# Row spreads and the memory decay as one rounded product over high and low parts, gate copies ahead of the maxima

## The chip, the cores and the metric

One core of one Trainium2 chip runs the whole program. The time is the device time of one execution in microseconds (us). Engines: PE (TensorE, matrix products), DVE (VectorE), ACT (ScalarE), POOL (GpSimd), SP (SyncE, which only issues the loads of weights here). Products accumulate in PSUM; all other tiles lie in SBUF.

## The reference, cut to what matters

256 tokens and 256 context tokens, width 1024, float32. A first block: modulated norm, one wide projection, windowed attention beside an mLSTM memory, a gated merge, a convolved FFN. A second block: a "fox" (forgetting) attention and a stick-breaking attention, FFN, a convolutional mixer, FFN. What the change touches:

```
q = rope(rms_norm(aq, q_norm_w));  k = rope(rms_norm(ak, k_norm_w))      # first attention: 1/rms per head and token
dmat = b[t] - b[s] + i[s];  m_t = max(b + m, dmat.max());  s = (q k^T) * exp(dmat - m_t)    # mLSTM
q, k = rms_norm per head (second attention, fox and stick-breaking)
y = sigmoid(ga) * (att @ wa) + sigmoid(gm) * (ml @ wm)
```

An rms factor exists once per head and token, as a row of 256 (token) values on the partition of its head; it is needed on all 64 partitions of the head. The "memory decay" is, per head, direction and token, minus the running maximum of `i[s] - b[s]`, needed on all 128 partitions. Both spreads are made by a matrix product with a selecting 0/1 operand.

## The kernel before, in words

Every weight block (128x1024) is loaded by SP into a ring `raw`, split into a rounded high part `whi` by ACT (L1145) and a rounded low part `wlo` by POOL (L313, one tensor_tensor of 128x1024 that reads SBUF and writes SBUF). PE multiplies with three rounded (fp32r) matmuls in place of one exact product (L482 to L484). In the FFNs some of the low parts are made by DVE.

Each engine has one stream of instructions, written out by hand and ordered by semaphores.

The projection blocks are called q = 0 to 59 (`W_IN_JOBS`); blocks 20 to 27 are the attention's queries, 28 to 35 the output gates ("mo"), 36 to 43 "ga", 44 to 51 "gm". On PE, `gp_job(q)` makes a block's product in a PSUM bank; on ACT, `evac(q)` copies it away and then makes the next high part. All "mo" and all "gm" products use bank 0, so `gp_job` of one waits for `evac` of the one before it. On DVE, `evac(q)` of a query block is followed by `rotated`.

Stage "memory" (h = 0 to 4, about 190 to 252 us). PE: `decay_rows(h)` (L673, two exact f32 products of 256 columns), `ml_scores(h)` (L683), `gp_job(28+2h)`, `ml_values(h-1)` (L703), `gp_job(29+2h)`. DVE: exponents from the decay (L1796, L1799), products with the scores (L1806, L1810), then in h = 0 the rms rows (L1763 to L1765) and `make_spread` (L1743), in h = 3 a second `make_spread`, then `combine(h-1)` (L1773 to L1785). ACT: exponentials (L1283), `evac(28+2h)`, an exponential (L1286); from h = 1 on it waits for the end of `combine(h-1)`, squares its result twice (L1292) and only then does `evac(29+2h)`. `ml_scores(h)` waits for DVE's products of h-1.

Stage "first spreads" (252 to 290 us). PE for i = 0 to 9: `spread_first(i)` (L744, an exact f32 product, 512 columns for i < 2, else 256), from i = 2 on `gp_job(36+i-2)`, from i = 4 on two transposes (L727). DVE multiplies by the result (L1855).

Stage "attention" (16 steps st, 290 to 373 us). PE: scores (L770, L774), the "gm" product in the steps of `GM_AT` (1, 3, 5, 7, 9, 11, 15, 16), transposes of the step before (L785), in odd steps values (L796) and reciprocals (L807). DVE: maxima (L1870), copies (L1879), and in even steps the output (L1893), which waits for ACT's L1333. ACT in step st: two exponentials (L1322, L1324), `evac` of the "gm" block of step st-1 with its split, then in even steps L1333.

Stage "second heads" (660 to 820 us). DVE, after the norm: `make_spread(spread2)` and seven more small preparing operations (L2054 to L2060), each followed by a wait for its own end (`link`); then it copies the values out of PSUM (L2139) once PE has made them. PE for j = 0 to 15: `project(j)`, at j = 1 the forget gates, from j = 6 on `spread_rstd(j-6)` (L924, exact, 256 columns), from j = 1 on `head_sums(j-1)` (L914), from j = 8 on stick-breaking scores (L959, L960), from j = 9 on `sb_later` (L968 to L971). `head_sums(0)` waits for the four copies L2139; `project(2)` for DVE's copy of `project(0)` (L2160). `row_rstd(g)` on DVE (L1576 to L1580, with ACT's L1431 and L1434) makes the rms rows of four blocks at j = 5, 9, 13 and after the loop; `forget_sums` comes at j = 6. Afterwards come the fox heads (L1010 to L1016, maxima L2118, L2127, transposes L1028), with spreads 10 and 11 ahead of them and 12 to 15 among heads 2 and 3.

Of the kernel before, what the change touches and what calls it, by code (L numbers as in the profile page):

```python
# [12 lines left out]
P = 128  # L13
# [112 lines left out]
def build(nc, xc_d, ccol_d, params_d, const_d, const1_d, const2_d, wgate_d, wf_d, stream_d, out_d):  # L126
# [3 lines left out]
    with ctx:  # L130
# [25 lines left out]
        spr = NG[:, :, :].rearrange("p a t -> p (a t)")  # L156
# [75 lines left out]
        def wait_rest(eng, s):  # L232
# [13 lines left out]
            "spread_ready", "v_chain", "v_ones", "rot_fin", "rows_read", "c_across", "modb_done",  # L246
# [173 lines left out]
        turned_cos = [work[:, 1024 + 256 * i:1280 + 256 * i] for i in range(4)]  # L420
        def spread_of(rows, b):
            return KX[0:rows, C1_COS + P * b:C1_COS + P * b + P] if b < 5 else spr[0:rows, P * (b - 5):P * (b - 4)]
# [34 lines left out]
        spread2 = KX[:, C2_N:2 * C2_N]  # L457

        def fin_out(i):

            return PS[:, 4 + i % 2, T:2 * T] if i < 8 else PS[:, 0 if i < 12 else i % 2, 0:T]
# [18 lines left out]
        def _(pe):  # L480
# [183 lines left out]
            def decay_rows(h):  # L664

                if h >= 1:
                    pe.wait_ge(S["ctx_exp"], 4 * h)
                    pe.wait_ge(S["arg_done"], 4 * h)
                else:
                    pe.wait_ge(S["em_done"], 1)  # L670
                for d in range(2):
                    r = 32 * d + h
                    mm = pe.matmul(PS[:, 1, T * d:T * d + T], ident[0:36, r:r + 1].broadcast_to((36, P)),  # L673
                                   NG[0:36, 0, :], start=True, stop=True)
                mm.then_inc(S["bc_done"], 1)
# [56 lines left out]
            def spread_first(i):  # L732

                if i >= 2:
                    pe.wait_ge(S["qk_fin"], i - 1)
                else:
                    pe.wait_ge(S["spread_ready"], 2)
                    pe.wait_ge(S["rq_done"], 2)
                if i < 2:
                    rows, sel, n = ROWS[0:4, 256:768], spread_of(4, i), 2 * T  # L740
                else:
                    b = i - 2
                    rows, sel, n = ROWS[0:16, 0:256], spread_of(16, b), T
                pe.matmul(PS[:, 2 + i % 2, 0:n], sel, rows,  # L744
                          start=True, stop=True).then_inc(S["rstd_bc"], 1)
# [171 lines left out]
            def spread_rstd(i):  # L917

                g, b = i // 4, i % 4
                pe.wait_ge(S["rq_done"], 3 + g)  # L920
                pe.wait_ge(S["spread_ready"], 3)
                if i > 8:
                    pe.wait_ge(S["qk_fin"], 10 + fin_before(i) + 1)
                pe.matmul(fin_out(i), spread2[0:8, P * b:P * b + P], rr2[2 + g][0:8, :],  # L924
# [207 lines left out]
        def _(act):  # L1132
# [182 lines left out]
            for st in range(STEPS + 3):  # L1315
                if st < STEPS:
# [9 lines left out]
                if st - 1 in GM_AT:  # L1326
                    evac(GM0 + GM_AT[st - 1])
# [212 lines left out]
        def _(dve):  # L1540
# [7 lines left out]

            cos, sin = KX[:, C1_COS:C1_COS + T], KX[:, C1_SIN:C1_SIN + T]
# [174 lines left out]
            for q in range(MO):  # L1724
# [10 lines left out]
                if q > AQ:  # L1735
                    rotated(q - AQ + 1)
            rotated(9)
# [3 lines left out]
            def make_spread(to, first, blocks, n=16):  # L1741

                dve.tensor_copy(to[0:n, 0:P * blocks].rearrange("r (h d) -> r h d", d=HD),  # L1743
                                ident[0:n, 2 * first:2 * first + 2 * blocks].unsqueeze(2)
                                .broadcast_to((n, 2 * blocks, HD))).then_inc(S["spread_ready"], 1)
# [43 lines left out]
            for h in range(5):  # L1789
# [23 lines left out]
                if h == 0:  # L1813
                    row_norms()
                    make_spread(KX[:, C1_COS:C1_N], 0, 5)
                if h == 3:
                    make_spread(spr, 5, 3)
# [222 lines left out]
            def row_rstd(g):  # L2040
# [3 lines left out]
                dve.wait_ge(S["rq_done"], 3 + g)  # L2044

            make_spread(spread2, 0, 4, 8)
# [341 lines left out]
```

## Time and profile before

| | us |
|---|---|
| median of 3 runs (1326.45 to 1329.6) | 1327.8 |
| profiled execution | 1325.02 |
| its span, first to last instruction | 1323.2 |
| busy in the span: PE | 1266.8 |
| PE weight loads | 1155.2 |
| DVE | 785.6 |
| POOL | 701.9 |
| ACT | 629.3 |
| mean granted TensorE clock | 0.977 of full |

Busy times are sums over the span; times inside it are counted from its start. Granted clock 1.0 is 2.4 GHz, 0.5 is 1.2 GHz. An exact f32 matmul stands in the rows as two instructions (x2), a rounded one as one.

### The profile page before, as it was taken

The numbers are of one execution on the slowest core, as the hardware profiler recorded it, in microseconds if no ns is written. First come the engines' busy times: TensorE is split into PE (matmuls) and PEld (weight loads), VectorE is DVE, ScalarE is ACT, GpSimd is POOL, SyncE is SP. The second block draws the span as 40 slices with busy tenths as digits, with TensorE's granted clock in tenths as the row PEclk, the third lists the DMA queues.
The fourth block names the chain that finished last, engine by engine and source line by source line (L and its number), as shares of the span: only waits on it lengthen the run. The fifth ranks groups of instructions, "written<-read, shape, count | busy, mean of one in ns | idle before, by whom it ended". The sixth has DMA issues, their size and how long they took to land.

```text
span 1323.2 us, 24847 instructions
## 1 busy us (share of the span) xinstructions
PE 1266.8 (96%) x9248; PEld 1155.2 (87%) x9248; DVE 785.6 (59%) x1432; ACT 629.3 (48%) x1081; POOL 701.9 (53%) x299
## 2 busy tenths in 40 slices
PE   5789999999999899999898999999999999999999
PEld 1578888876699799999887857999999999999998
DVE  3688567535631467776546652577776424677775
ACT  3523343454543655555634522655555644654553
POOL 1536663252248555557585301655558787655564
PEclk9899999999999899999999977999999999999999
DMA  9568662141135444556463300455546456355552
GB/s 373 199 229 272 242 195 80 49 128 49 49 93 164 127 161 176 187 190 217 127 191 112 93 20 5 140 190 190 180 176 218 148 187 190 129 189 190 189 179 78
DMA packets 57739, 208.45 MB, mean 158 GB/s; under 512 B 6576, under 2 KB 7600, under 8 KB 57408
## 3 DMA queue, kind: packets, MB, share of 16 engines
q1 hardware_dynamic: 57168, 205.55, 46.2%
q0 software_dynamic: 496, 1.87, 0.4%
q8 instruction: 50, 0.82, 0.2%
q14 instruction: 25, 0.20, 0.1%
HBM read 206.35 MB, written 1.05 MB: 157 GB/s over the span
## 4 chain that ended last, share of the span: by engine, by line
PE 88%; DVE 6%; DMA 3%; issue 2%; ACT 2%; SPq 0%; DVEq 0%; ACTq 0%
PE ps L482 24%; PE ps L483 23%; PE ps L484 23%; DMA raw<-in_stream 3%; PE ps L703 2%; PE ps L517 2%; PE ps L519 2%; PE ps L520 2%; PE ps L547 1%; PE ps L796 1%; PE ps L1016 1%; PE ps L770 1%; DVE raw L1645 1%; PE ps L924 1%; PE ps L785 1%
## 5 line engine op out<-in xcount | busy, mean ns | idle before, releaser
L313 POOL TENSOR_TENSOR wlo<-raw,whi 128x1024 fp32r<-128x1024 f32 x286 | 696.1, 2451 | 583.1 <-ACT whi L1145 557.1
L482 PE MATMUL ps<-Hh,whi 128*128 128x256 f32 (+2 forms) x1976 | 577.6, 292 | 20.2 <-DVE Hl L1611 4.7
L483 PE MATMUL ps<-Hl,whi 128*128 128x256 f32 (+2 forms) x1976 | 568.7, 288 | 0.0
L484 PE MATMUL ps<-Hh,wlo 128*128 128x256 f32 (+2 forms) x1976 | 568.5, 288 | 0.0
L482 PEld LDWEIGHTS ps<-Hh,whi 128*128 128x128 f32 (+1 forms) x1976 | 382.0, 193 | 34.1 <-issue 14.9
L1145 ACT ACTIVATE whi<-raw 128x1024 fp32r<-128x1024 f32 x338 | 353.3, 1052 | 114.4 <-DMA raw<-in_stream 57.2
L483 PEld LDWEIGHTS ps<-Hl,whi 128*128 128x128 f32 (+1 forms) x1976 | 382.3, 193 | 3.1
L484 PEld LDWEIGHTS ps<-Hh,wlo 128*128 128x128 f32 (+1 forms) x1976 | 382.0, 193 | 2.7
L2000 DVE SCALAR_TENSOR_TENSOR arena<-ps,sm,arena 128x255 f32<-128x255 f32 (+1 forms) x264 | 127.4, 483 | 103.8 <-ACT arena L1395 95.9
L482 PE MATMUL ps<-dh,whi 128*128 128x256 f32 x592 | 167.6, 283 | 1.1 <-DVE dl L1912 1.1
L483 PE MATMUL ps<-dl,whi 128*128 128x256 f32 x592 | 167.5, 283 | 0.0
L484 PE MATMUL ps<-dh,wlo 128*128 128x256 f32 x592 | 167.5, 283 | 0.0
L1395 ACT ACTIVATE arena<-ps,sm 128x256 f32<-128x256 f32 x132 | 66.7, 505 | 134.5 <-DVE ps L1990 104.1
L482 PEld LDWEIGHTS ps<-dh,whi 128*128 128x128 f32 x592 | 113.7, 192 | 1.3 <-issue 1.3
L483 PEld LDWEIGHTS ps<-dl,whi 128*128 128x128 f32 x592 | 113.7, 192 | 0.0
L484 PEld LDWEIGHTS ps<-dh,wlo 128*128 128x128 f32 x592 | 113.7, 192 | 0.0
L1962 DVE COPY sm<-params 128x8 f32 (+1 forms) x66 | 89.1, 1355 | 7.9 <-DVE arena L2000 7.6
L1973 DVE TENSOR_TENSOR wlo<-raw,whi 128x1024 fp32r<-128x1024 f32 x52 | 81.0, 1557 | 1.5
L1406 ACT ACTIVATE dh<-ps 128x256 fp32r<-128x256 f32 x60 | 23.1, 385 | 100.7 <-DVE ps L2009 100.7
L1645 DVE SCALAR_TENSOR_TENSOR raw<-raw,arena 128x1024 f32<-128x1024 f32 x32 | 57.7, 1830 | 3.9 <-DMA raw<-in_stream 3.6
L517 PE MATMUL ps<-whi,Hh 128*128 128x512 f32 (+1 forms) x128 | 47.4, 370 | 4.0 <-DVE Hl L1632 4.0
L519 PE MATMUL ps<-whi,Hl 128*128 128x512 f32 (+1 forms) x128 | 47.2, 368 | 0.0
(298 smaller groups left out, 1249.0 us busy)
## 6 DMA issues: line engine op xcount, KB each, us to landing
raw<-in_stream SPq DMA_DIRECT2D x386, 512.0 KB, 4.1
X<-in_xc SPq DMA_DIRECT2D x2, 1024.0 KB, 10.4
out_y<-X SPq DMA_DIRECT2D x8, 128.0 KB, 2.0
kx<-in_const POOLq DMA_DIRECT2D x1, 512.0 KB, 7.0
arena<-in_wgate POOLq DMA_DIRECT2D x1, 400.0 KB, 8.9
params<-in_params POOLq DMA_DIRECT2D x1, 372.0 KB, 6.9
k<-in_const POOLq DMA_DIRECT2D x1, 256.0 KB, 4.9
kx<-in_const POOLq DMA_DIRECT2D x1, 256.0 KB, 4.6
```

The costliest lines, as they stand in the source:

```text
L313: pool.tensor_tensor(wlo[:, slot, :], raw[:, rslot, :], whi[:, slot, :].bitcast(f32), ALU.subtract).then_inc(rest_done[0], 1)
L482: pe.matmul(out, lh, rh, start=start, stop=False, skip_group_check=True)
L483: pe.matmul(out, lh, rl, start=False, stop=False, skip_group_check=True)
L484: return pe.matmul(out, ll, rh, start=False, stop=stop, skip_group_check=True)
L517: pe.matmul(out, Hh[:, k, tok], wh_, start=k == 0 and first, stop=False, skip_group_check=True)
L519: pe.matmul(out, Hl[:, k, tok], wh_, start=False, stop=False, skip_group_check=True)
L1145: act.activation(whi[:, s % RING, :], raw[:, r % RING, :], ACT.Copy).then_inc(hi_done, 1)
L1395: act.activation(tc, PS[:, 4 + 2 * slot + j, 0:T], ACT.Identity, bias=bias, scale=cwb[:, slot, 3 * j:3 * j + 1]).then_inc(S["centre"], 1)
L1645: dve.scalar_tensor_tensor(raw[:, r % RING, :], raw[:, r % RING, :], 1.0, c_across, ALU.mult, ALU.mult, accum_out=MODB[:, at:at + 1]).then ...
L1962: dve.tensor_copy(cwb[:, i % 2, :], src).then_inc(S["cw_copy"], 1)
L1973: dve.tensor_tensor(wlo[:, s % RING, :], raw[:, RAW_OF_W[s] % RING, :], whi[:, s % RING, :].bitcast(f32), ALU.subtract).then_inc(rest_done ...
L2000: dve.scalar_tensor_tensor(tc[:, lo:hi], u[:, src:src + hi - lo], cwb[:, slot, 3 * j + 1 + n:3 * j + 2 + n], tc[:, lo:hi], ALU.mult, ALU.a ...
```

## The change

Three things. (1) Row operands of the three kinds of spreads are split by DVE into a rounded high part and the rounded rest, stacked on two groups of partitions of a cleared fp32r tile, and the selecting operand is doubled likewise, so that each spread is one rounded product. (2) For this, DVE clears and fills tiles: two clears, three copies and a subtract in query block 21; three clears, two copies and two subtracts in h = 0; in h = 1 and h = 2 two clears, four copies and a small memset each, ahead of `combine`; ahead of the second heads six clears and four copies in place of one copy; a copy and a subtract behind each `row_rstd`. `cleared`, and all copies except those of `spread_rows`, wait for their own end. (3) ACT's `evac` of a "gm" block stands ahead of the two exponentials of its step.

```diff
+        decay, decay_of = Hl[0:100, 4, T:2 * T], Hh[0:100, 3, T:T + 36]
+        k_rows, q_rows = Hl[0:36, 5:7, T:2 * T], Hl[0:48, 7, T:2 * T]
         def spread_of(rows, b):
-            return KX[0:rows, C1_COS + P * b:C1_COS + P * b + P] if b < 5 else spr[0:rows, P * (b - 5):P * (b - 4)]
+            return Hh[0:rows, 4 + b // 2, T + P * (b % 2):T + P * (b % 2) + P]
...
-        spread2 = KX[:, C2_N:2 * C2_N]
+        head_rows = [dh[0:40, 0, :], dh[0:40, 1, :], dl[0:40, 0, :], dl[0:40, 1, :]]
+        spread2 = [Hl[0:40, k, T:2 * T] for k in (0, 3)]
...
-                    pe.wait_ge(S["em_done"], 1)
+                    pe.wait_ge(S["decay_split"], 1)
...
-                    mm = pe.matmul(PS[:, 1, T * d:T * d + T], ident[0:36, r:r + 1].broadcast_to((36, P)),
-                                   NG[0:36, 0, :], start=True, stop=True)
+                    mm = pe.matmul(PS[:, 1, T * d:T * d + T], decay_of[:, r:r + 1].broadcast_to((100, P)),
+                                   decay, start=True, stop=True)
...
-                    pe.wait_ge(S["rq_done"], 2)
+                    pe.wait_ge(S["rows_split"], 2)
...
-                pe.wait_ge(S["rq_done"], 3 + g)
-                pe.wait_ge(S["spread_ready"], 3)
+                pe.wait_ge(S["heads_split"], 1 + g)
+                pe.wait_ge(S["spread_ready"], 6)
...
-                pe.matmul(fin_out(i), spread2[0:8, P * b:P * b + P], rr2[2 + g][0:8, :],
+                pe.matmul(fin_out(i), spread2[b // 2][:, P * (b % 2):P * (b % 2) + P], head_rows[g],
...
             for st in range(STEPS + 3):
+                if st - 1 in GM_AT:
+                    evac(GM0 + GM_AT[st - 1])
                 if st < STEPS:
...
-                if st - 1 in GM_AT:
-                    evac(GM0 + GM_AT[st - 1])
...
+            def cleared(out, like):
+                link(dve.tensor_scalar(out, like, 0.0, None, ALU.mult))
+            def spread_rows(rows, out, heads):
+                n = heads.stop - heads.start
+                dve.tensor_copy(out.rearrange("r (h d) -> r h d", d=HD),
+                                ident[rows, heads].unsqueeze(2).broadcast_to((rows.stop - rows.start, n, HD)))\
+                   .then_inc(S["spread_ready"], 1)
+            def split_rows(hi, lo, rows, done):
+                link(dve.tensor_copy(hi, rows))
+                dve.tensor_tensor(lo, rows, hi.bitcast(f32), ALU.subtract).then_inc(done, 1)
...
+                if q == AQ + 1:
+                    cleared(decay, K0[0:100, 0:T])
+                    cleared(decay_of, K0[0:100, 0:36])
+                    for rows in (slice(0, 36), slice(64, 100)):
+                        link(dve.tensor_copy(decay_of[rows, :], ident[rows, rows]))
+                    split_rows(decay[0:36, :], decay[64:100, :], NG[0:36, 0, :], S["decay_split"])
...
                 if h == 0:
                     row_norms()
-                    make_spread(KX[:, C1_COS:C1_N], 0, 5)
-                if h == 3:
-                    make_spread(spr, 5, 3)
+                    for k in (5, 6, 7):
+                        cleared(Hl[0:48, k, T:2 * T], K0[0:48, 0:T])
+                    for to, src in (((Hl[r, 5:7, T:2 * T] for r in (slice(0, 4), slice(32, 36))),
+                                     ROWS[0:4, 256:768].rearrange("r (b t) -> r b t", b=2)),
+                                    ((Hl[r, 7, T:2 * T] for r in (slice(0, 16), slice(32, 48))), ROWS[0:16, 0:256])):
+                        split_rows(*to, src, S["rows_split"])
+                if 1 <= h <= 2:
+                    for k in (2 * h + 2, 2 * h + 3):
+                        cleared(Hh[0:48, k, T:2 * T], K0[0:48, 0:T])
+                        for rows in (slice(0, 16), slice(32, 48)):
+                            at = rows.start + 4 * (k - 4)
+                            link(dve.tensor_copy(Hh[rows, k, T:2 * T].rearrange("r (h d) -> r h d", d=HD),
+                                                 ident[rows, at:at + 4].unsqueeze(2).broadcast_to((16, 4, HD))))
+                    dve.memset(rows_read, 0.0).then_inc(S["spread_ready"], 1)
                 if h >= 1:
                     combine(h - 1)
...
                 dve.wait_ge(S["rq_done"], 3 + g)
-
-            make_spread(spread2, 0, 4, 8)
+                split_rows(head_rows[g][0:8, :], head_rows[g][32:40, :], rr2[2 + g][0:8, :], S["heads_split"])
+
+            for out in (*head_rows, *spread2):
+                cleared(out, K0[0:40, 0:T])
+            for i in range(2):
+                for at in (0, 32):
+                    spread_rows(slice(at, at + 8), spread2[i][at:at + 8, :], slice(at + 4 * i, at + 4 * i + 4))
```

## Rows read from the trace of the kernel before

**Rows 1.** The page: the chain that ended last, by engine.
```profile
PE 88%; DVE 6%; DMA 3%; issue 2%; ACT 2%; SPq 0%; DVEq 0%; ACTq 0%
```

**Rows 2.** The chain in order of time: start us, us, what.
```profile
217.23 1.92 PE ps L683 x8
...
260.40 0.62 PE ps L744 x2
...
315.08 0.12 PE ps L484
```

**Rows 3.** Timeline of DVE, PE and POOL, 660 to 690 us: start, duration, instruction, [idle before].
```profile
660.63 2.36 DVE L2056 CAST Hh<-k 8x8 fp32r<-8x8 f32 x1
667.80 4.81 DVE L2060 TENSOR_SCALAR Hh<-k 128x256 fp32r<-128x256 f32 x2
678.95 2.48 DVE L2139 COPY arena<-ps 128x512 f32<-128x512 f32 x4 [6.34 <-PE ps L520]
...
687.25 0.60 PE L914 MATMUL ps<-arena,k 128*8 128x256 f32 x2
...
660.57 28.45 POOL L313 TENSOR_TENSOR wlo<-raw,whi 128x1024 fp32r<-128x1024 f32 x12 [14.22 <-ACT whi L1145]
```

**Rows 4.** Timeline of DVE, all operands in SBUF, POOL idle (708, 712, 200 us).
```profile
708.31 0.28 DVE L2071 TENSOR_SCALAR arena<-arena 8x256 f32<-8x256 f32 x1
711.79 0.41 DVE L2075 TENSOR_TENSOR Hh<-arena,Hh 8x256 fp32r<-8x256 f32 x1
...
200.83 0.68 DVE L1764 TENSOR_TENSOR arena<-arena 4x512 f32<-4x512 f32 x1
```

**Rows 5.** Timeline of the memory stage, 203 to 220 us.
```profile
204.09 0.39 PE L482 MATMUL ps<-Hh,whi 128*128 128x256 f32 x1 [1.10 <-ACT arena L1237]
...
203.60 0.48 DVE L1743 COPY kx<-k 16x640 f32<-16x640 f32 x1
...
215.09 0.87 DVE L1785 SCALAR_TENSOR_TENSOR X<-ps,sm,X 128x256 f32<-128x256 f32 x2
...
216.95 0.36 ACT L1237 ACTIVATE arena<-ps 128x256 f32<-128x256 f32 x1
```

**Rows 6.** Windows: busy us of PE, PEld, DVE, ACT, POOL, then granted clock.
```profile
651.30:655.10 3.80, 0.00 (x0) 0.00 (x0) 3.07 (x8) 1.63 (x4) 0.00 (x0) 1.00 0.00 0
656.40:659.60 3.20, 3.20 (x10) 2.48 (x8) 3.06 (x10) 1.95 (x6) 0.00 (x0) 0.53 0.00 0
775.00:790.00 15.00, 15.00 (x50) 10.28 (x50) 6.33 (x18) 2.32 (x11) 0.00 (x0) 0.52 0.01 2
```

**Rows 7.** Waits of PE, 290 to 372 us: who waited for whom, us, times, longest.
```profile
PE ps L482 <- ACT arena L1237: 2.7, 5, 0.5
PE ps L796 <- DVE arena L1893: 1.4, 1, 1.4
```

**Rows 8.** Timeline of ACT, attention, 320 to 325 us.
```profile
320.89 0.69 ACT L1322 ACTIVATE arena<-ps,sm 128x512 f32<-128x512 f32 x1 [4.26 <-DVE rows L1870]
...
322.87 1.06 ACT L1145 ACTIVATE whi<-raw 128x1024 fp32r<-128x1024 f32 x1
```

**Rows 9.** Timeline of PE, DVE and POOL, second heads, 706 to 728 us.
```profile
713.36 0.36 PE L482 MATMUL ps<-Hh,whi 128*128 128x256 f32 x1 [1.48 <-DVE arena L2160]
...
725.71 0.67 PE L968 MATMUL ps<-arena,kx 128*128 128x256 f32 x2 [0.70 <-DVE arena L2091]
...
725.01 0.55 DVE L2091 TENSOR_TENSOR arena<-arena,kx 128x384 f32<-128x384 f32 x1
...
725.13 2.68 POOL L313 TENSOR_TENSOR wlo<-raw,whi 128x1024 fp32r<-128x1024 f32 x1 [2.65 <-ACT whi L1145]
```

**Rows 10.** The chain: spreads 12 and 13 of the fox heads.
```profile
780.15 2.00 PE ps L924 x4
```

**Rows 11.** Timeline of PE, a later fox head.
```profile
799.20 0.90 PE L1028 MATMUL ps<-k,arena 128*128 128x128 f32 x3 [1.37 <-DVE arena L2127]
```

**Rows 12.** Timeline of DVE, query block 22.
```profile
168.54 0.48 DVE L1712 SCALAR_TENSOR_TENSOR arena<-ps,sm,kx 128x256 f32<-128x256 f32 x1 [1.21 <-ACT arena L1246]
```

More of the change, by code:

```diff
@@ L155, in build @@
         NG = sb("ng", [P, 2, T])
-        spr = NG[:, :, :].rearrange("p a t -> p (a t)")
         PS = ctx.enter_context(nc.psum_tensor("ps", [P, 8, 512], f32))
@@ L245, in build @@
             "sb_arg", "sb_wm", "fox_max", "fox_pt", "fox_even", "t2_lo", "mix_cu", "fin", "wg_lo",
-            "spread_ready", "v_chain", "v_ones", "rot_fin", "rows_read", "c_across", "modb_done",
+            "spread_ready", "decay_split", "rows_split", "heads_split", "v_chain", "v_ones", "rot_fin", "rows_read", "c_across", "modb_done",
             "c_bc", "mod_t", "mod_copy", "ss_ready", "gates_ps", "u_t", "st_done", "bc_done", "qk_done", "pv_done", "rot_done", "rstd_bc", "sc_done",
@@ L737, in spread_first @@
                     pe.wait_ge(S["spread_ready"], 2)
-                    pe.wait_ge(S["rq_done"], 2)
+                    pe.wait_ge(S["rows_split"], 2)
                 if i < 2:
-                    rows, sel, n = ROWS[0:4, 256:768], spread_of(4, i), 2 * T
+                    rows, sel, n = k_rows, spread_of(36, i), 2 * T
                 else:
                     b = i - 2
-                    rows, sel, n = ROWS[0:16, 0:256], spread_of(16, b), T
+                    rows, sel, n = q_rows, spread_of(48, b), T
                 pe.matmul(PS[:, 2 + i % 2, 0:n], sel, rows,
@@ L1739, in _ @@
             dve.tensor_tensor(MODB[:, :], MODB[:, :], pr("b_mod", 2 * KC, 6 * KC), ALU.add).then_inc(S["modb_done"], 1)
[L1741 to L1745, printed above, removed]
             ROW_SETS = ((4, 7, 2 * T, 256), (16, 6, T, 0))
```

## The prediction

> **What bounds the kernel now.** I read the chain that ended last by engine, then PE's waits, then the timelines around every edit. PE holds 88% of the chain [rows 1]; it is the bound nearly everywhere, and a product taken from it is worth its own length. The exceptions are a few places where PE waits for DVE, and every edit that adds to DVE must be read against those. Two things decide this case. First, DVE operations whose operands all lie in SBUF do not run while POOL makes a low part: an 8x8 copy took 2.36 us, and two clears of 128x256 took 4.81, all inside an unbroken run of 12 POOL operations (28.45 us, 2.37 each) [rows 3]; the same kinds take 0.28 to 0.68 us with POOL idle [rows 4]. Second, after PE stood idle for 3.8 us the granted clock fell to 0.53 in the stretch that followed, the 1.2 GHz level, against 1.0 [rows 6].
>
> **Part 1, what a spread saves.** An exact spread of 256 columns holds PE for 0.62 us on the chain, a rounded matmul of 256 columns for 0.12 [rows 2]. One change of operand type more or less goes with it, so between exact neighbours I take 0.41 saved. Where both neighbours are rounded (spreads 2 and 3 of the first attention) I take 0.69. Bounds for each: 0.31 (half of the exact product saved) and 0.69.
>
> **Part 2, query block 21.** DVE gets a clear, a small clear, two small copies, a copy and a subtract: about 1.3 us unblocked by rows 4. DVE has 1.21 us idle before the next block's first operation [rows 12]. At least one POOL operation (2.4 us) lies in the way. PE needs that block's copy some 3 us after it is normally made. I take +0.6; bounds 0 (one POOL operation) and +3.0 (two more).
>
> **Part 3, the memory stage.** The decay product of h = 0 saves nothing: the scores behind it wait for DVE's last rotation anyhow. That of h = 1 saves nothing either: PE waits 1.10 us at 204.09 for a copy of ACT that waits for the rms rows of DVE [rows 5]. Those of h = 2 and 3 save 0.8 each. Against this, DVE in h = 0 gets three clears at 0.31 (0.93), a copy of 512 (0.4), a subtract of 512 (0.7), a copy (0.3) and a subtract (0.4), less the removed copy (0.4 to the next operation): +2.4, with the links +2.7. The block by a POOL operation that the stage has anyway only changes its place. In h = 1 come two clears and four copies at 0.31: 1.9, and 0.6 for the rest of a POOL operation that is under way then. So `combine(0)`, whose last operations begin at 215.09, comes 2.7 + 2.5 = 5.2 us later. Behind it on ACT stand two squares and `evac(31)`, which comes at 216.95 [rows 5], and PE's block 32 waits for that. PE reached block 32 at 219.15 (217.23 + 1.92, [rows 2]), so the copy, done at 217.3, had 1.8 us to spare. Net +3.4 at block 32, and PE stands idle 3.7 us there. The same pattern in h = 2 has the lateness of DVE (again 1.9 more, less the 2 us it waited for PE) against a PE that is late itself: I keep +3.2 in all, the savings of h = 2 and 3 taken up by the waits. Bounds: -1.6 (all additions hidden, two decays saved) and +6 (a further POOL operation in the way twice, less half). For the idle 3.7 us I add 1.6 of low clock, the 3.2 us of rows 6 at half speed; bounds 0 and 3.2.
>
> **Part 4, first spreads.** Spreads 0 and 1 stand beside a chain of DVE (combine, multiply) and save nothing. Spreads 2 to 9 stand on the path: 6 x 0.41 + 2 x 0.69 = -3.8. Cover: DVE (0.4 to 1.3 us) and POOL (2.4) have under 3 us of work per block of 3.9. Bounds -2.5 and -5.0. The make_spread removed in h = 3 is off the path.
>
> **Part 5, gate copies.** PE waited five times, 2.7 us in all, for the copy out of bank 0, and once 1.4 us for L1893 [rows 7], which stood behind ACT's L1333, which stood behind the copy and its split. ACT is idle 4.26 us ahead of the exponentials of an even step; the copy and split take about 1.3 [rows 8], and the product they wait for is done by then. Both waits go, of the second 1.2, since DVE is ready for L1893 only 0.2 earlier than PE needs it: -2.7 - 1.2 = -3.9. Next to come late is nothing: with them gone PE is busy all through. Bounds -4.1 and, should a copy wait for its product and hold the exponentials back, +1.3 once.
>
> **Part 6, ahead of the second heads.** This is the largest term. DVE reaches the place at 659.91. Before, eight small operations followed, two of the seven linked ones ahead of POOL's run, five blocked; they ended at 672.6, and DVE then stood idle 6.34 us until the value products were ready at 678.95 [rows 3]. Now there are 17: three clears pass before POOL starts at 660.57; three clears, four copies and the old seven operations, 14 in all, meet a run of 12 POOL operations. One passes behind each POOL operation (five rows in a row show it): 12 x 2.39 = 28.7 us from 660.8, then two unblocked, so DVE is free at about 690.0. The four copies L2139 take 2.48 [rows 3], so `head_sums(0)` starts at 692.5 instead of 687.25: +5.2. If the four unlinked copies pass together, 11 are blocked, and it is +2.7 (no row shows unlinked ones under a run of POOL; one by one is the nearest, rows 3, and I take it). Bounds: 0 and +7. PE idle for 5.2 us brings the low clock again: +1.6, bounds 0 and +3.2.
>
> The Trainium skill, page "SBUF — State Buffer", section "Who interferes with whom", says that DVE and GpSimd share one pair of SBUF ports as an exclusive lock, taken for a whole instruction by whichever issues first, by DVE's copy, cast and tensor_scalar when everything is in SBUF and by a two-input operation against a GpSimd operation that reads. The trace agrees, down to the 8x8 copy of 2.36 us. A reader who took only the sizes of the added operations (some 3 us in all at this place) would find them hidden under the 6.34 us of idle time, and the sum below would be 6.8 lower.
>
> **Part 7, spreads of the second heads.** (a) j = 5, 6: DVE's chain from the first rms rows to L2160 sets PE's start at 713.36, a wait of 1.48 [rows 9]. A copy and a subtract, 0.3 + 0.41, lie on it: +0.8. The shift can put the last operations of `forget_sums` behind the next POOL operation: then +3.3. These are within 0.1 us of each other, so I take +2.1. (b) j = 9: PE waits 0.70 for L2091, which starts at 725.01, 0.12 ahead of a POOL operation; pushed 0.7 later, with POOL's start pulled ahead by the shorter spread, it falls behind it and ends 1.65 later [rows 9]: +1.65, bounds +0.3 and +2.4. (c) Spreads 4 to 9: 6 x -0.41 = -2.5, and +0.2 for j = 13, where DVE had 0.9 us to spare: -2.3, bounds -3.5 and -0.5. (d) Spreads 10 to 15: 10 saves 0.4; the fourth split adds 0.7 ahead of the first maxima; 12 and 13 hold PE 2.00 at 1.2 GHz [rows 10] and save 1.45; 14 and 15 covered a latency that elsewhere shows as a wait of 1.37 [rows 11], so they save 2.0 - 1.37 = 0.6. Sum -1.8, bounds -3.5 and 0.
>
> **Sum.** 0.6 + 3.2 + 1.6 - 3.8 - 3.9 + 5.2 + 1.6 + 2.1 + 1.65 - 2.3 - 1.8 = +4.15. The profiled execution took 1325.0 (span 1323.2 and 1.8 around it); it becomes 1329.2. It lay 2.8 below the median of 1327.8, so the median becomes 1332.0.
>
> **Rivals.**
> (A) DVE's additions are hidden: parts 3 and 6 cost nothing, because operations slip in between POOL's or their order in time turns out luckier. For it: DVE is busy only 59% of the span, and 6.34 us are idle in front of L2139. Against it: five operations in a row that did not slip in. It decides where DVE is free before 678.95, some 7 blocked operations after 660.57, instead of 14. Price: part 6 gone (-6.8), part 3 at -1.6 instead of +4.8 (-6.4): 1332.0 - 13.2 = 1318.8. This is the case on the faster side.
> (B) Half of it: the unlinked copies pass together (-2.5) and no low clock follows the stall in the memory stage (-1.6): 1327.9, no change.
> (C) The races with POOL go badly: part 7a at 3.3 (+1.2), part 2 at 3.0 (+2.4), low clock twice as long in both stalls (+3.2): 1338.8. For it: every DVE operation in SBUF is exposed to POOL's 2.4 us.
> (D) The gate copies do not help, since ACT waits in them for products or raw blocks: part 5 at 0 with the rest as forecast: 1335.9. Against it: 4.26 us idle at the place.
>
> **How the numbers follow.** Forecast 0.45, A 0.20, B 0.17, C 0.13, D 0.05. The likeliest is 1332.0, its own range 1328.5 to 1336. The range for 8 in 10 reaches down to A and up towards C: 1319 to 1338. A difference under 0.2%, 2.7 us, is what a measurement of this kernel can't tell from none. Slower: C, D and nearly nine tenths of the forecast, 0.57; same: B's most part and the rest of the forecast, 0.21; faster: A and a little of B, 0.22.
>
> **What would show it.** Right: L744, L673 and L924 as single instructions; no wait of L482 for L1237 among the attention's steps; a wait of PE of about 3.7 us for L1237 near 219 us; DVE operations of 2.4 us in unbroken order from 660 to 689 us, L2139 near 690 and a wait of `head_sums` of about 5 us; granted clock 0.5 behind both. Wrong: L2139 still at 679, `evac(31)` before PE reaches block 32, or added DVE operations of 0.3 us during POOL's. Parts 4 and 5 are wrong if the stretches 255 to 290 and 297 to 372 us do not shorten by 3.8 and 3.9.

## The result and the profile after

The changed kernel took 1332.24 us (median of 8 runs, 1330.07 to 1334.29); the kernel before, beside it, 1326.91 (8 runs, 1323.62 to 1329.60). The ratio is 1.0042, with a 95% interval of 1.0029 to 1.0055: slower by 0.4%. The forecast was 1332.0. It was a change of +4.15 put on a kernel of 1327.8, the median of three executions; measured side by side the change is +5.3. The profiled execution took 1330.07, with a span of 1327.8 against 1323.2. It is the fastest of the eight: its mean granted clock is 0.971, that of the others 0.964 to 0.969.

The chain of the page, by engine, now reads (to [rows 1]):

```profile
PE 84%; DVE 10%; DMA 3%; issue 2%; ACT 1%; SPq 0%; DVEq 0%; ACTq 0%
```

DVE's part of it grew from 6% to 10% and PE's fell from 88% to 84%: PE's products got shorter, and its waits for DVE longer. To place it, I took the start of the same PE instruction in both traces and noted how much later (+) the changed kernel is there:

| stretch (us of the span before) | later at its start | at its end | change | forecast |
|---|---|---|---|---|
| query block 21 (168 to 173) | -0.22 | +0.74 | +0.96 | +0.6 |
| memory stage (191 to 252) | +0.72 | +4.73 | +4.0 | +4.8 |
| first spreads (252 to 289) | +4.73 | +0.73 | -4.0 | -3.8 |
| attention (289 to 359) | +0.73 | -4.27 | -5.0 | -3.9 |
| ahead of the second heads (648 to 691) | -4.46 | +2.64 | +7.1 | +6.8 |
| second heads, j = 4 to 8 (7a) | +2.64 | +1.28 | -1.4 | +2.1 |
| j = 9 (7b) | +1.28 | +5.19 | +3.9 | +1.65 |
| j = 10 to 15 (7c) | +5.19 | +3.69 | -1.5 | -2.3 |
| the fox heads (7d) | +3.69 | +3.71 | 0.0 | -1.8 |

The last 0.9 us lie behind the last product, mostly in the output's transfers, which the change doesn't touch: from that product's start to the end of the span it is 4.4 us instead of 3.6.

**Ahead of the second heads.** The timelines of DVE, PE and POOL, changed kernel, 655 to 689 us (start, duration, instruction, idle before it; to [rows 3]):

```profile
655.46 0.60 DVE L1554 TENSOR_SCALAR dh<-k 40x256 fp32r<-40x256 f32 x2
656.09 2.70 DVE L1554 TENSOR_SCALAR dl<-k 40x256 fp32r<-40x256 f32 x2
658.83 4.78 DVE L1554 TENSOR_SCALAR Hl<-k 40x256 fp32r<-40x256 f32 x2
663.65 9.60 DVE L1559 CAST Hl<-k 8x256 fp32r<-8x256 f32 x4
...
685.67 2.48 DVE L2175 COPY arena<-ps 128x512 f32<-128x512 f32 x4
...
688.31 1.01 PE L917 MATMUL ps<-arena,k 128*8 128x256 f32 x2 [5.49 <-DVE arena L2175]
...
656.11 28.79 POOL L312 TENSOR_TENSOR wlo<-raw,whi 128x1024 fp32r<-128x1024 f32 x12 [14.23 <-ACT whi L1148]
```

Three clears pass at 0.3 us; from 656.4 on each clear, copy and rounding takes 2.3 to 2.4, the length of one POOL operation. The four copies, which don't wait for each other's end, do so too (9.60). Of the 14 operations that remained 12 were held, one per POOL operation, and the last two took 0.3 each. The copy out of the value banks starts at 685.67, not at 678.95 - 4.46 = 674.5, and PE stands 5.49 us. The windows behind it (busy time of PE, PEld, DVE, ACT and POOL, then the granted clock) show the 1.2 GHz level and the return to 2.4:

```profile
688.30:691.50 3.20, 3.19 (x12) 2.35 (x13) 0.52 (x2) 0.00 (x0) 0.00 (x0) 0.50 0.03 14
692.00:695.20 3.20, 3.20 (x25) 2.63 (x25) 0.42 (x1) 1.33 (x2) 0.20 (x1) 1.00 0.00 0
```

The head sums of j = 0 come 5.52 us later against before than the projections, those of j = 1 another 1.58.

**The memory stage.** The same timelines at 216 to 224 us (to [rows 5]):

```profile
216.91 0.80 DVE L1554 TENSOR_SCALAR Hh<-k 48x256 fp32r<-48x256 f32 x1
...
219.45 0.16 DVE L1793 SCALAR_TENSOR_TENSOR sm<-ps,emT 128x4 f32<-128x4 f32 x1
220.85 0.87 DVE L1805 SCALAR_TENSOR_TENSOR X<-ps,sm,X 128x256 f32<-128x256 f32 x2
...
222.70 0.36 ACT L1240 ACTIVATE arena<-ps 128x256 f32<-128x256 f32 x1
...
223.12 0.38 PE L485 MATMUL ps<-Hh,whi 128*128 128x256 f32 x1 [3.84 <-ACT arena L1240]
```

The clears and constant copies of h = 1 stand in front of `combine(0)`; its last operations begin at 220.85, not 215.09, and ACT's copy out of block 31's bank at 222.70, not 216.95: 5.8 later (forecast 5.2). PE's block 32 starts at 223.12 instead of 218.80, 4.3 later: it had 1.5 us to spare.

**First spreads.** The chain of the changed kernel has one such piece per spread of 256 columns (start, us, what):

```profile
263.32 0.31 PE ps L747
277.49 0.31 PE ps L747
```

A window between the third and the fourth spread, of the kernel before:

```profile
257.00:259.00 2.00, 2.00 (x11) 2.00 (x11) 2.00 (x4) 1.97 (x2) 0.00 (x0) 0.50 0.00 0
```

The same stretch of the changed kernel:

```profile
260.00:262.00 2.00, 2.00 (x16) 1.87 (x17) 1.83 (x7) 1.94 (x4) 0.00 (x0) 1.00 0.03 8
```

And of experiment 2, whose code up to this place is the changed kernel's:

```profile
261.00:264.00 3.00, 3.00 (x14) 2.87 (x15) 2.83 (x8) 2.94 (x4) 0.00 (x0) 0.56 0.00 0
```

A rounded spread holds PE 0.31 us where the exact one held it 0.62 [rows 2], so each saves 0.31: from the third spread to the tenth the distance to the kernel before changes by just that, eight times. Between the third and the fourth it changes by another 1.5: before, a stretch at 1.2 GHz lay there, and in the profiled execution of the changed kernel it doesn't. That is no effect of the change. Of the twelve kernels profiled for this document eleven have the stretch, among them experiments 2, 4 and 10, which up to there are the changed kernel, with the same wait of PE in front (2.7 us in all four).

**Attention.** PE's waits (290 to 372 us before, 290 to 368 us changed; to [rows 7]; who waited for whom, us, times, longest): the five waits for the copy out of bank 0 are gone, and so is the one for L1893. The first row is the kernel before, which had the wait for the first queries too; the second is the changed kernel's only row.

```profile
PE ps L770 <- DVE Hl L1843: 1.5, 1, 1.5
PE ps L773 <- DVE Hl L1874: 1.5, 1, 1.5
```

**The second heads.** Timelines of PE, DVE and POOL, changed kernel, 716 to 730 us (to [rows 9]):

```profile
716.76 0.35 PE L485 MATMUL ps<-Hh,whi 128*128 128x256 f32 x1 [2.10 <-DVE arena L2196]
...
729.33 1.04 PE L971 MATMUL ps<-arena,kx 128*128 128x256 f32 x2 [3.03 <-DVE arena L2127]
...
727.37 1.81 DVE L2127 TENSOR_TENSOR arena<-arena,kx 128x384 f32<-128x384 f32 x1
...
726.41 2.35 POOL L312 TENSOR_TENSOR wlo<-raw,whi 128x1024 fp32r<-128x1024 f32 x1 [2.34 <-ACT whi L1148]
```

Windows of the kernel before:

```profile
713.00:716.40 3.40, 3.04 (x17) 3.07 (x18) 0.98 (x3) 0.00 (x0) 2.23 (x1) 0.66 0.39 133
716.40:719.00 2.60, 2.60 (x13) 1.74 (x12) 0.00 (x0) 0.33 (x2) 0.00 (x0) 0.79 0.53 189
```

Windows of the changed kernel, the same place and behind the wait of j = 9:

```profile
713.00:716.40 3.40, 1.66 (x10) 0.90 (x9) 3.18 (x7) 1.33 (x2) 2.02 (x2) 1.00 0.28 88
...
729.00:732.60 3.60, 3.27 (x14) 3.13 (x15) 2.24 (x6) 0.52 (x1) 0.00 (x0) 0.57 0.45 146
```

DVE reaches its operation at j = 9 (L2127) 0.96 us behind POOL's start, where before it was 0.12 ahead; PE's wait grows from 0.70 to 3.03. The stretch of low clock that before lay at 713 to 719 is absent, and one follows the new wait at 729. The absence is again not the change's doing: experiments 2 and 3, which at this place have the changed kernel's code and its wait of 2.10, have the stretch. In experiment 1, which here is the kernel before, it comes some microseconds earlier (granted 0.52 from 704 to 706), ahead of the wait for DVE, and costs PE nothing. The stretch at 729 stands behind each of the seven waits of 3.0 us that were profiled at j = 9.

### The profile page after: what moved, and what is told of

The parts are those of the page before. It is cut to its first block, busy times and chain, and to the rows that moved or that the text cites. A ratio compares the mean times of both kernels' runs of the same rounds, so it can differ in the third digit from the quotient of the medians.

```text
span 1327.8 us, 24817 instructions
## 1 busy us (share of the span) xinstructions
PE 1253.7 (94%) x9214; PEld 1150.7 (87%) x9214; DVE 819.6 (62%) x1474; ACT 629.0 (47%) x1081; POOL 700.4 (53%) x299
## 3 DMA queue, kind: packets, MB, share of 16 engines
q0 software_dynamic: 496, 1.87, 0.3%
## 4 chain that ended last, share of the span: by engine, by line
PE 84%; DVE 10%; DMA 3%; issue 2%; ACT 1%; SPq 0%; DVEq 0%; ACTq 0%
PE ps L485 23%; PE ps L486 23%; PE ps L487 22%; DMA raw<-in_stream 3%; PE ps L706 1%; PE ps L550 1%; PE ps L773 1%; PE ps L799 1%; PE ps L520 1%; PE ps L523 1%; PE ps L522 1%; PE ps L788 1%; PE ps L1019 1%; DVE raw L1664 1%; DVE Hl L1559 1%
```

## The experiments

My theory: two costs, each a wait for DVE's added work, ahead of the second heads (5.5 us and 1.6 of low clock) and in the memory stage (3.8 and 1.6), and a third at j = 9; the gate copies gain 5 us, the spreads 0.31 each. The rivals: the waits have another releaser, or the added work is hidden as its size suggests. Ratios are against the kernel before, timed beside each.

**1. The gate copies alone, in the kernel before.**
```
 step(st) of ACT:
+    if st - 1 in GM_AT: evac(GM0 + GM_AT[st - 1])
     ... (the maxima's part)
-    if st - 1 in GM_AT: evac(GM0 + GM_AT[st - 1])
```


> The kernel before with the gate copies ahead of the exponentials and nothing else. Theory: PE's five waits for the copy out of bank 0 (0.5 us each, and 0.2 us for the first product after each) and the 1.4 us wait for the output both go, as between the traces of before and after, where this stretch became 5.0 us shorter: 1321.9 us, 5.0 below the kernel before; the trace of 290 to 372 us has no wait of PE for ACT's copy. The forecast's own term was 3.9 us. Rival: the stretch gained only because the spreads ahead of it had changed its start against the loads and low parts; then alone it gives under 2 us.

Measured 1321.65, ratio 0.9965 (0.9951 to 0.9978). In the attention the place against before moves from +0.31 to -4.66: -5.0, all of what the changed kernel gains there. PE's waits, 290 to 368 us:

```profile
PE ps L770 <- DVE Hl L1843: 1.5, 1, 1.5
```

So this edit alone makes the kernel faster, and the rest of the change costs some 10 us. Of the 5.0 the profiled span keeps 3.6: at j = 9 this kernel loses 1.5 us to a stretch of low clock (-5.18 to -3.65), in code that its edit doesn't touch.

**2. The second heads' preparation spread over j = 1 to 4** (in the changed kernel).
```
-            for out in (*head_rows, *spread2): cleared(out, ...)
-            for i in range(2): for at in (0, 32): spread_rows(...)
+            def prepare_heads(j):      # called behind the copy of q2 in step j
+                if j in (1, 2): three of the six clears
+                if j in (3, 4): two of the four spread_rows
```


> The changed kernel with the preparation of the second heads (six clears, four copies) moved from ahead of the seven old operations to behind the copies of projections 1 to 4. Theory: the seven linked operations then end near 670 us as before, the copies L2139 start when the value products are ready (about 674 us in this kernel's time), the 5.5 us wait of head_sums and 1.6 us of low clock behind it go: 1325.1 us, 7.1 below the changed kernel's 1332.2. Rival (moved, not gone): behind projections 1 to 4 the ten operations meet the same low parts and the copies of projections come late, so PE waits there instead: 1329 or more.

Measured 1326.09, ratio 0.9992 (0.9983 to 1.0001). PE's waits of 640 to 700 us are one row:

```profile
PE ps L520 <- DVE Hl L1651: 4.0, 1, 4.0
```

The window behind the head sums:

```profile
687.00:691.00 4.00, 4.00 (x31) 3.44 (x31) 2.01 (x6) 1.33 (x2) 0.72 (x2) 1.00 0.60 216
```

The head sums' wait is gone, and with it the low clock: from 648 to 691 us the place against before stays at -1.9. The same ten operations cost 7.1 us at the one place and nothing there when moved: it was their position, not their amount. The whole kernel gains 6.1 over the changed one, a little less than the 7.1 expected.

**3. `combine(h - 1)` ahead of the constants in the memory stage**, and the row splits of h = 0 moved to h = 3.
```
+                if h >= 1: combine(h - 1)
                 if 1 <= h <= 2: ... clears and copies ...
-                if h >= 1: combine(h - 1)
```


> The changed kernel with the memory stage's fills moved: those of h = 1 and 2 behind combine, that of h = 0 to h = 3 behind combine(2). Theory: PE's wait of 3.8 us for the copy of block 31, the low clock behind it (1.2 to 1.6 us) and the smaller waits go, and the decays of h = 2 and 3 are saved: the stage ends 4.9 to 5.6 us earlier, 1326.6 to 1327.3 us. Rival: the fill in h = 0 is what made DVE late and any place before the exponentials of the next head costs the same, or the fill of h = 3 makes the first spreads wait: 1330 or more.

Measured 1328.25, ratio 1.0012 (1.0002 to 1.0021). The stage costs -0.1 us (+0.41 to +0.28) instead of +4.0. PE's waits, 200 to 260 us, of the changed kernel and then of this one:

```profile
PE ps L485 <- ACT arena L1240: 6.1, 3, 3.8
```
```profile
PE ps L485 <- ACT arena L1240: 2.1, 1, 2.1
```

The kernel gains 4.0 us, less than the 4.9 to 5.6 expected. The wait of 2.1 is that of block 30 at 204.5, which the changed kernel has as well (2.11); here a stretch of low clock followed it (granted 0.50 from 205.5 to 208.5), in the changed kernel's profile none.

**4. Is the 1.6 us behind the stall the clock?** The changed kernel with 36 products into a free bank in front of the head sums of j = 0; their result is read by nobody. DVE, and what PE waits for, is as it was.
```
+    if j == 1:
+        for _ in range(36): pe.matmul(PS[:, 6, 0:T], Hh[:, 4, 0:P], Hh[:, 5, 0:T], ...)
```


> The changed kernel with 36 rounded products of 256 columns (4.3 us at full clock) into an unused PSUM bank ahead of head_sums(0), inside its wait of 5.5 us; they compute nothing that is used. Theory of the clock: PE doesn't stand idle there, the granted clock stays 1.0 behind it, and the 1.6 us between 688 and 694 us come back: 1330.6 us. Rival: the 1.6 us is not the clock but DVE's lateness, or the clock falls at another place instead: 1332.2 us or more.

Measured 1330.16, ratio 1.0027 (1.0016 to 1.0039). PE's timeline and a window behind it:

```profile
685.83 4.48 PE L1071 MATMUL ps<-Hh 128*128 128x256 f32 x36
690.84 0.59 PE L917 MATMUL ps<-arena,k 128*8 128x256 f32 x2 [0.54 <-DVE arena L2179]
```
```profile
687.00:691.00 4.00, 3.46 (x29) 3.22 (x28) 3.90 (x9) 0.00 (x0) 0.44 (x1) 1.00 0.74 228
```

The head sums come as late as before (5.56 against 5.52 us later than the projections), but the clock stays at 1.00 and the next ones lose nothing (0.0 instead of 1.58). The price of the low clock at this place is shown, apart from the wait's. The whole kernel is 2.1 us below the changed one, near the forecast, though the two intervals overlap.

**5. Both moves together.**


> The changed kernel with both moves at once: combine(h - 1) ahead of the clears and splits in the memory stage (and the rows of spreads 5 to 7 split in h = 3), and the clears and constant copies of the second heads behind j = 1 to 4. Theory (the two stretches are independent, each move gives back what it gave alone, 6.2 and 4.0 us): 1332.2 - 10.2 = 1322.0, faster than before by 0.37%. Rival (a part of the gain of the one is what the other waits for, or the granted clock falls elsewhere): 1324 to 1326, no difference from before.

Measured 1319.08, ratio 0.9945 (0.9931 to 0.9959): 0.97% below the changed kernel, about 13 us, where the sum of the two alone is 10.6 (0.50% and 0.30%). The difference is inside the intervals, which are 2 us wide to either side. Its profiled execution is at the top of its six times, 1323.2, with a mean clock of 0.968 where those of 1317 to 1319 have 0.971 to 0.974. So the moves add up; that they help each other is not shown.

**6. The splits of the rstd rows later** (both moves, and splits of heads 1 and 2 behind j = 9 and 13, the last one behind the first `fox_even`).
```
             def row_rstd(g):
                 ...
-                split_rows(head_rows[g]...)      # for g = 1, 2, 3
+                if j in (9, 13): split_heads((j - 5) // 4)    # end of step j
+                if h == 1: split_heads(3)                      # behind fox_even(0)
```


> As the kernel with both moves, and the splits of the rstd rows of heads 1 and 2 behind j = 9 and 13, not in the step that makes the rows, and that of head 3 behind the first maxima of the forget head. Theory (the splits delay DVE's rms rows, which delay PE at j = 9 by 3.0 us, with a low clock behind it, and ahead of the last spreads): 3 to 4 us faster than with both moves alone, about 1318. Rival (the split stands on the path wherever it is put, since the spread needs it): within 1 us of both moves alone, 1321 to 1323.

Measured 1320.23, ratio 0.9948 (0.9931 to 0.9965): no gain, so the theory that the splits delay j = 9 fell. DVE, PE and POOL at j = 9:

```profile
720.37 2.57 DVE L2138 TENSOR_TENSOR arena<-arena,kx 128x384 f32<-128x384 f32 x1
...
723.09 1.19 PE L971 MATMUL ps<-arena,kx 128*128 128x256 f32 x2 [3.03 <-DVE arena L2138]
...
720.18 2.35 POOL L312 TENSOR_TENSOR wlo<-raw,whi 128x1024 fp32r<-128x1024 f32 x1 [2.35 <-ACT whi L1148]
```

DVE is where it was in the kernel before, 2.06 us behind the start of spread 3 (before: 725.01 - 722.94 = 2.07). POOL starts 1.87 us behind it, not 2.19. Its low part waits for ACT's high part, and that stands behind a squaring which waits for the spread itself. ACT, of the kernel before and of this one (spreads at 722.94 and 718.31):

```profile
723.72 0.38 ACT L1491 ACTIVATE arena<-ps 128x256 f32<-128x256 f32 x1 [1.45 <-PE ps L924]
```
```profile
718.77 0.38 ACT L1494 ACTIVATE arena<-ps 128x256 f32<-128x256 f32 x1 [1.14 <-PE ps L927]
```

The squaring follows the spread's start by 0.46 instead of 0.78, since the rounded spread is 0.31 shorter. The other profiles say the same: POOL starts 2.18 to 2.19 behind the spread in the three kernels with exact spreads, and 1.87 in all nine with rounded ones. DVE now loses by 0.19 us what it won by 0.12, and pays 2 us for it. So the shorter spread is what moves POOL's start, and with it the wait. That gave the next kernel.

**7. The terms first at j = 9** (kernel 6, with one more edit).
```
-                if 7 <= j: finish_qk(j - 7)
+                if 7 <= j and j != 9: finish_qk(j - 7)
                 ... sb_exponents, sb_terms ...
+                if j == 9: finish_qk(2)
```


> The kernel with both moves and late splits, and at j = 9 finish_qk(2) behind sb_terms(0), not ahead of it; all else is the same. In the kernel with late splits DVE reached its operation on the third terms 0.19 us behind the start of a POOL operation and took 2.57 us for it instead of 0.55. Theory (PE's 3.0 us wait at j = 9 is a race with POOL, lost because the shorter spread lets POOL start 0.32 earlier, and not the work that the splits add): with DVE 0.40 earlier the race is won, the operation takes 0.55, the wait falls from 3.0 to 0.6, and the kernel is 2.4 us faster than with late splits, 1317 to 1318; a stretch of low clock behind it may go too (1.6 more). Rival (POOL starts from the same cause as DVE and holds it again): the wait stays at 3.0 and the time at 1320.

Measured 1313.47, ratio 0.9909 (0.9893 to 0.9924). DVE, PE and POOL:

```profile
718.59 0.55 DVE L2138 TENSOR_TENSOR arena<-arena,kx 128x384 f32<-128x384 f32 x1
...
719.29 0.67 PE L971 MATMUL ps<-arena,kx 128*128 128x256 f32 x2 [0.61 <-DVE arena L2138]
...
718.79 2.60 POOL L312 TENSOR_TENSOR wlo<-raw,whi 128x1024 fp32r<-128x1024 f32 x1 [2.34 <-ACT whi L1148]
```

DVE is 0.20 us ahead, takes 0.55, and the wait falls from 3.03 to 0.61. From the head sums of j = 8 to spread 4 kernel 6 loses 4.6 us against the kernel before (-4.95 to -0.34), this one gains 0.1 (-6.34 to -6.41): 2.4 is the race, the rest a stretch of low clock that followed the wait. The kernel gains 6.8 us by the medians and 5.2 by the ratios, more than the forecast of 1317 to 1318. Part of it is that stretch; another (1.2 us, ahead of the second heads) is longer in kernel 6's profile than in this one's.

**8. The rows last** (kernel 7, and the fourth `row_rstd` with its split behind `fox_even(0)`).
```
             finish_qk(11)
-            row_rstd(3)
             for h in range(1, 12):
                 ... if 1 <= h < 9: fox_even(h - 1)
+                if h == 1: row_rstd(3); split_heads(3)
```


> As the kernel with the terms first, and the fourth row_rstd with its split behind fox_even(0) instead of ahead of the maxima of the forget head 0. Theory (PE's wait of 2.9 us for the first normalized weights is DVE's work in front of them, 1.8 us of it the rstd rows; the spreads that need the rows come some 5 us later): the wait falls to about 1.1, and the kernel is 1.8 us faster than with the terms first. Rival (the spreads of heads 12 to 15 then wait for the rows by as much): no difference from the terms first.

Measured 1312.98, ratio 0.9890 (0.9871 to 0.9909). PE's waits, 600 to 850 us, of kernel 7 and then of this one:

```profile
PE ps L1031 <- DVE arena L2174: 7.0, 4, 2.9
```
```profile
PE ps L1031 <- DVE arena L2174: 5.5, 4, 1.4
```

The longest wait falls from 2.9 to 1.4 and the place gains 1.55, near the theory's 1.8. Over the whole kernel that can't be told from no gain: the two intervals overlap, and the two profiled spans are equal (1314.4 and 1314.3), since this execution lost about 1.1 us to a longer stretch of low clock ahead of the second heads.

**9. Only the added work, in the kernel before.** Six clears and three small copies ahead of the second heads, nothing else.
```
+            for out in (six 40x256 tiles): link(dve.tensor_scalar(out, K0[0:40, 0:T], 0.0, None, ALU.mult))
+            for i in range(3): dve.tensor_copy(8x256 of constants)
```


> The kernel before with nothing but DVE work added ahead of the second heads: six clears of 40x256 and three copies of 8x256, linked or counted as the changed kernel has them; their outputs are written again later, so nothing else changes. Run alone these nine would take some 3 us, against 6.34 us in which DVE stood idle there. Theory (one of them passes behind each POOL operation of 2.4 us): PE waits 4 to 5.5 us for the head sums, with 1.6 us of low clock behind it, so 1326.9 + 6 to 7 = 1333 to 1334. Rival (by size they are hidden under the idle time): 1326.9, no change.

Measured 1334.54, ratio 1.0058 (1.0042 to 1.0074): 7.7 us for nine operations which, at 0.30 each, have 2.7 us of work, at a place where DVE stood idle for 6.34 [rows 3]. DVE's timeline:

```profile
660.96 0.60 DVE L2049 TENSOR_SCALAR dh<-k 40x256 fp32r<-40x256 f32 x2
661.60 4.79 DVE L2049 TENSOR_SCALAR dl<-k 40x256 fp32r<-40x256 f32 x2
666.42 4.77 DVE L2049 TENSOR_SCALAR Hl<-k 40x256 fp32r<-40x256 f32 x2
671.23 4.79 DVE L2051 CAST dh<-k 8x256 fp32r<-8x256 f32 x2
```

PE then waits for the head sums:

```profile
693.49 1.01 PE L914 MATMUL ps<-arena,k 128*8 128x256 f32 x2 [5.45 <-DVE arena L2147]
```

The granted clock behind it is 0.50 (693.5 to 696.7), and the place moves by 7.4 from 648 to 691 us. Rival A, the hidden work, is refuted here by itself.

**10. The clears as memset** (the changed kernel).
```
-                link(dve.tensor_scalar(out, like, 0.0, None, ALU.mult))
+                link(dve.memset(out.bitcast(f32), 0.0))
```


> The changed kernel with the six clears ahead of the second heads written as a memset of zero in place of a tensor_scalar times zero that reads the constants; nothing else is changed. If a memset, which reads nothing from SBUF, runs beside POOL's operations: 11 operations are held instead of 14, the three clears take 0.3 to 0.5 us each, the wait ahead of the head sums falls from 5.5 to under 1 us: 1332.2 - 5 - 1.6 = about 1326. If it is held as any other: the rows stay at 2.4 us each, 1332.2. Between them (11 operations still meet the run, and the copies set the end): a wait of 2 to 3 us, 1328 to 1330.

Measured 1327.97, ratio 1.0013 (1.0004 to 1.0023): 0.29% or 3.9 us below the changed kernel. DVE, PE and POOL:

```profile
658.62 0.66 DVE L2079 MEMSET dl<- 40x256 f32 x2
659.38 0.66 DVE L2079 MEMSET Hl<- 40x256 f32 x2
660.07 8.13 DVE L1559 CAST Hl<-k 8x256 fp32r<-8x256 f32 x4
...
658.42 28.59 POOL L312 TENSOR_TENSOR wlo<-raw,whi 128x1024 fp32r<-128x1024 f32 x12 [14.26 <-ACT whi L1148]
```

Four memsets pass within POOL's first operation at 0.33 each; the copies behind them, which read constants, are held again. The wait is 2.3 instead of 5.5, the middle case of the expectation, and a stretch of low clock still follows it:

```profile
687.47 0.59 PE L917 MATMUL ps<-arena,k 128*8 128x256 f32 x2 [2.28 <-DVE arena L2175]
688.50:691.80 3.30, 3.30 (x17) 3.30 (x17) 0.00 (x0) 0.00 (x0) 0.00 (x0) 0.50 0.39 143
```

The Trainium skill, page "SBUF — State Buffer", section "Who interferes with whom", says that a DVE instruction with at most one input from SBUF and outside the two-port modes doesn't contend with GpSimd; for the memset the trace agrees (0.33 us).

## Why the prediction was right, and where it wasn't

- **Parts 3 and 6, the two stalls**: right in mechanism, place and size. Forecast waits 3.7 and 5.2 us, measured 3.84 and 5.49; forecast costs 4.8 and 6.8, measured 4.0 and 7.1. What decided it was to count operations (14 that meet the run, 12 of them held, at 2.39 each) and not their sizes; experiment 9 shows that count alone. In part 3 DVE was 5.8 late, not 5.2, and PE had 1.5 us to spare, not 1.8: its block 32 began at 218.80 in the kernel before, not at 219.15. Experiments 2 and 3 show that each stall goes with the operations' position, and experiment 4 that the 1.6 us behind the second is the clock.
- **The unlinked copies** passed one by one (9.60 for four), as chosen; the choice was between +2.7 and +5.2.
- **Part 2**: +0.96 against +0.6; no run tested it by itself.
- **Part 5**: -5.0 instead of -3.9. The waits went as said, but each took 0.75 with it, not 0.53. Before, the product behind such a wait started 0.98 us after the one ahead of it, which the rows give 0.44 of length; without the wait it starts after 0.28, overlapping it, and its successor follows after 0.16 instead of 0.22. Five times 0.22 is the miss. That PE would be "busy all through" was wrong: a wait of 1.5 us for DVE's L1843 stood there before and stays, unchanged, so it didn't touch the sum.
- **Part 4**: -4.0 against -3.8, but not by its reason. A spread saves 0.31, the lower bound, not 0.41 or 0.69; eight of them make -2.5. The surcharge for a change of operand type, from which 0.41 and 0.69 came, is shown by no run: spreads with rounded products on both sides save the same 0.31, and the first product behind a spread takes 0.32 in both kernels. The other 1.5 is the stretch of low clock behind the third spread, which only the changed kernel's profiled execution lacks. That is luck.
- **Part 7a** failed in sign (-1.4, forecast +2.1). The wait grew by 0.62, about the 0.8 of the copy and subtract, and the further POOL operation didn't come in between. Two spreads in this stretch, which the sum left out, saved 0.31 each. The remaining 1.5 is the low clock before (0.66 and 0.79 at 713 to 719), which comes and goes between executions; without it this part of the kernel is level.
- **Part 7b** was right in mechanism (the race with POOL was lost) and too small: +3.9 against +1.65. The wait alone grew 2.33, at its upper bound of 2.4; 1.6 is the low clock behind it. It named two causes, the splits and the shorter spread; experiment 6 takes the first away and the wait stays, so the second is enough alone, and experiment 7 shows that the wait is the race.
- **Parts 7c and 7d**: -1.5 and 0.0 against -2.3 and -1.8. Again 0.31 per spread, not 0.41. In 7d the added split lies in front of the first maxima: PE's wait for the first weights grew from 2.67 to 3.70, and the low clock ends 1.2 us later.

The time met the result to 0.2 us partly by luck. The misses of 7a and 7b (-3.5, +2.3), 5 (-1.1), 7c and 7d (+2.6) cancel, and the change, forecast at +4.15 and measured at +5.3, was put on a median of three executions, 1327.8, that lies 0.9 above the one of eight. Low clock is in three of the four errors above 1 us (1.5 of 7a's, 1.6 of 7b's, 1.2 of 7d's); the prediction had it only in parts 3 and 6. Between the two profiles three stretches came (223, 688 and 729 us) and two went (257 and 713), 1.5 to 1.6 us each. The three stand behind new waits of 3.0 us and more, and in every profile that has such a wait at one of these places the clock falls within some microseconds of it. The two that went belong to the execution, not to the kernel.

Of the rivals, A is refuted by experiment 9, D by experiment 1. B's first half, that the unlinked copies pass together, is refuted by the 9.60 us of the four. B had also said that the low clock might not follow the stall in the memory stage; the place there shows 5.4 us between the last score product ahead of it and the values (+0.22 to +5.60), 3.84 of wait and 1.5 more, so it did. C was not seen: block 21 cost 0.96, 7a had no further POOL operation, and no stall had more than 1.6 us of low clock behind it.

What stays open: why single executions of one kernel differ by up to 6 us (1317.2 to 1323.2 in experiment 5). Their mean clocks differ too, 0.968 to 0.974. The profiles show that low stretches come and go at the same place behind the same wait: none follows the wait of 2.69 us ahead of the third spread in the changed kernel's profile, and one follows it in the eight others with rounded spreads. Behind the 2.11 at 204 there is one in seven of these nine. What makes them do so wasn't tried. It also means that a sum over the places of two profiles carries an error of 1.5 us for each such stretch.

## What to carry to other kernels

Beside a run of GpSimd operations like this one, count VectorE's operations in SBUF, not their microseconds: each that met the run cost the length of one GpSimd operation here (2.4 us), so nine of 0.3 us cost 7 us where 6 were free. Put constants where no such run is under way, or write zeros with a memset. A gain on the critical engine moves the start of everything that it releases; where two other engines hold each other up and start within some tenths of a microsecond, that can turn the order round. Here a product shorter by 0.3 made a wait longer by 2.3, with low clock behind it, and swapping two independent operations in front of the race brought it back (1320 to 1313). Before a gain or loss of 1.5 us in a profile is put down to an edit, see whether it is a stretch of low clock, and whether other profiles of the same code have it.

## What the hardware showed that I had not expected

- A run of 12 POOL operations lets one DVE operation through behind each, whether or not a semaphore links DVE's operations (9.60 us for four unlinked 8x256 copies).
- A memset on DVE runs beside POOL at 0.33 us; a `tensor_scalar` times zero of the same tile takes 2.4.
- A rounded product of 256 columns holds the chain 0.31 us as a spread, behind exact transposes (277.49) and between rounded products (263.32) alike, though 0.12 in a block's run [rows 2]: of the 0.50 between the single durations, 0.31 is saved.
- A stretch of 1.2 GHz may or may not follow the same wait at the same place: behind 2.11 us at 204 in seven of nine profiles, behind 2.69 us ahead of the third spread in eight of nine.
- When a wait of 0.53 us goes, PE gets back 0.75.
